# A delta-rule scan in three threads, with crosswise operands and a block-diagonal intermediate

## The chip, the cores and the metric

One core of one Trainium2 chip runs the whole program. The metric is the device time of one execution in microseconds (us). Times of single instructions are in nanoseconds (ns) or us, as the rows give them.

## The reference, cut to what matters

The reference is a network of several layers. The change lies in one part of its first block, a recurrence ("delta rule") over 256 context tokens and then 2048 tokens, for 6 heads of 64 and in two directions:

```python
def step(S, inp):
    w_t, k_t, v_t, kk_t, a_t = inp[:5]
    sa = jnp.einsum('bhvk,bhk->bhv', S, kk_t)
    S = (S * w_t[:, :, None, :] - sa[..., None] * (kk_t * a_t)[:, :, None, :]
         + v_t[..., None] * k_t[:, :, None, :])
    y = jnp.einsum('bhvk,bhk->bhv', S, inp[5]) if emit else None
    return S, y
state, ys = lax.scan(step, state, xs)
```

The state S is a 64 by 64 matrix for each head and direction. The second direction reads the tokens from the end. All numbers are fp32.

## The kernel before

`rwkv_scan` does the recurrence in 18 steps (2 of context, without output, then 16 with output). A step handles 128 tokens as two chunks of 64, for six units `u`: three groups `g` of two heads, each in two directions. Six inputs of a unit (scaled identity, alpha, rho, beta, kappa, v) lie in a tile `X`. The stages of a step, and the names used below:

- **turned** and **grams** (the fronts), once for each unit of the next step: four transposes of full 128 by 128 tiles into `gram`, a copy out by ScalarE (L1728), then 12 or 16 products of 64-row operands into `gram`, and one masked copy out by VectorE (L1759). GpSimd prepares `XE` (L1571) and the start `W` of the inverse (L1583).
- **z** and **n**, five rounds for each group: the inverse of a triangular 64 by 64 matrix for each chunk, head and direction grows by doubling. z multiplies the Gram matrix by the transposed inverse (8 matmuls of 64 by 64, 16 in the first round), ScalarE copies the result out (L1735), n multiplies that by the inverse (8 matmuls of 64 by 64, and in rounds 1 to 4 four more that make the transposed result of direction 1). VectorE writes the new entries into `W` through a mask (L1771, L1772) and transposes the other direction with one instruction (L1774).
- **x**, **p**, **f**, **s**, for each group: the solved vectors (8 matmuls with 128 moving columns), the transition matrices and gains (8 with 128 columns and 32 of 64 by 64), then the state and output of the first and of the second chunk (8 each).

`walk` sets one order for all engines: `PHASES` is the list z1 n1 z2 n2 ... z5 n5 x p f s; in each phase the three groups follow one another, and the fronts of the next step are put in at phases 0, 2, 4, 6, 8 and 9 (`AHEAD`). So a step's x, p, f and s run with nothing of the next step's rounds beside them. Each group has a PSUM pair `db[g]` of its own, and `gram` is a fourth pair shared by the fronts and the gains. The tensor engine's program is unrolled: a step is some 588 matmuls and 24 transposes. The trace shows each fp32 matmul as two pairs of LDWEIGHTS and MATMUL and each transpose as one pair. In the trace every matmul of the scan has line L1608 (the helper `mm`) and every transpose L1618.

In the rows, PE is the tensor engine's matmul, PEld its weight load; "64*64" is the part of the array that the stationary operand takes (rows*columns), and "64x128" after it is the moving operand.

Of the kernel before, what the change touches and what calls it, by code (L numbers as in the profile page):

```python
# [14 lines left out]
P = 128  # L15
# [1421 lines left out]
def rwkv_scan(nc, R, E, masks, levels, eye, ident, YR):  # L1437
# [7 lines left out]
    X_I, X_AL, X_RH, X_BE, X_KA, X_V = range(6)  # L1445
    K_AL, K_BE, K_KA, K_V, K_A, K_AR, K_KL, K_KR, K_AT, K_S0, K_Z, K_W0 = 0, 1, 2, 3, 4, 5, 6, 7, 8, 9, 10, 11
# [3 lines left out]
    PHASES = [(w, b) for b in range(1, LV) for w in "zn"] + [("x", 0), ("p", 0), ("f", 0), ("s", 0)]  # L1450
    AHEAD = {0: 0, 2: 1, 4: 2, 6: 3, 8: 4, 9: 5}

    PRODS, EVACS = 15, 18

    with ExitStack() as ctx:
        s = Scope(nc, ctx, "rsc")
        X = [[s.sb(f"X{b}{u}", [P, 6, P]) for u in range(NU)] for b in range(2)]
        XE = [s.sb(f"XE{b}", [P, 2, P]) for b in range(2)]
        TK = [[s.sb(f"TK{b}{g}", [P, 12, 2, P]) for g in range(NG)] for b in range(2)]
        W = [[s.sb(f"W{b}{g}", [P, 2, 2, P]) for g in range(NG)] for b in range(2)]  # L1460
        X12 = [s.sb(f"X12{g}", [P, 2, 2, 2, HD]) for g in range(NG)]
        PQ = [s.sb(f"PQ{g}", [P, 2, 2, 2, HD]) for g in range(NG)]
        GY = [s.sb(f"GY{g}", [P, 2, 2, 2, HD]) for g in range(NG)]
        Y = [s.sb(f"Y{g}", [P, 2, 2, HD]) for g in range(NG)]
        S = [[s.sb(f"S{a}{g}", [P, 2, HD]) for g in range(NG)] for a in range(2)]
# [4 lines left out]
        e = s.sb("e", [P, NU, 2 * CH])  # L1470
        gram = ctx.enter_context(nc.psum_tensor("rsc_gram", [P, 2, NT], F32))
        db = [ctx.enter_context(nc.psum_tensor(f"rsc_db{g}", [P, 2, NT], F32)) for g in range(NG)]
        const_in, zeroed = s.sem("const_in"), s.sem("zeroed")
        x_in = [s.sems(f"x_in{b}", NU) for b in range(2)]
        xe_ready, tl_full, tl_done, gram_full, m4_done, s0_ready, start_ready = (
            s.sem(n) for n in ("xe_ready", "tl_full", "tl_done", "gram_full", "m4_done", "s0_ready", "start_ready"))
        prod, evac, gy_done, y_out = (s.sems(n, NG) for n in ("prod", "evac", "gy_done", "y_out"))

        def scan(step):

            for n in range(NS):
                step(n // 2, n % 2, n >= NCX)

        def after(k, b):

            return None if k == NLT // 2 and b == 1 else ((k, 1) if b == 0 else (k + 1, 0))

        def walk(k, b, emit, phase, turned, grams):

            nxt = after(k, b)  # L1490
            for i, (w, lev) in enumerate(PHASES):
                for g in range(NG):
                    phase(k, b, emit, w, lev, g)
                    if nxt and i in AHEAD and g == 0:
                        turned(*nxt, AHEAD[i])
                if nxt and i in AHEAD:
                    grams(*nxt, AHEAD[i])

# [4 lines left out]
        def rows_of(u, t):  # L1503

            return t if u == 0 else other(t)

        def alpha_rho(x, h, u, cp):

            flat = x[HEADS[h], :, :].rearrange("p a t -> p (a t)")
            if u % 2 == 0:  # L1510
                return x[HEADS[h], X_AL:X_RH + 1, CHUNKS[cp]]
            if cp == 0:
                return flat[:, X_AL * P + C:X_AL * P + 3 * C].rearrange("p (a t) -> p a t", a=2)
            return flat[:, X_AL * P:X_AL * P + 6 * C].rearrange("p (a t) -> p a t", a=2)[:, :, 0:C]

        with nc.Block() as block:
            @block.sync
            def _(sp):
                def load(b, u, src):
                    x = X[b][u]  # L1520
                    if u % 2 == 0:
                        sp.dma_start(x[:, X_AL:, :], src).then_inc(x_in[b][u], 16)
                        return
                    sp.dma_start(x[:, X_RH:, :], src[:, 1:, :]).then_inc(x_in[b][u], 16)
                    for t in CHUNKS:
                        sp.dma_start(x[:, X_AL, other(t)], src[:, 0, t]).then_inc(x_in[b][u], 16)

                for dst, src in ((mk, masks), (lv, levels), (ey, eye), (idn, ident), (e, E)):
                    sp.dma_start(dst[:], src).then_inc(const_in, 16)
                for b in range(2):  # L1530
                    for u in range(NU):
                        m, d = divmod(u, 2)
                        c = NLT + b if d == 0 else NS - 1 - b
                        load(b, u, R[c, m, d])

                def step(k, b, emit):
                    if k < NLT // 2:
                        for u in range(NU):
                            m, d = divmod(u, 2)
                            c = k * 2 + b if d == 0 else k * -2 + (NLT - 1 - b)  # L1540
                            if d == 0:
                                sp.wait_ge(evac[m], k * (2 * EVACS) + (b * EVACS + 16))
                            load(b, u, R[c, m, d])
                    if emit:
                        for g in range(NG):
                            sp.wait_ge(evac[g], k * (2 * EVACS) + (b + 1) * EVACS)
                            for d in range(2):
                                tok = k * (2 * P) + (b - 2) * P if d == 0 else k * (-2 * P) + (NS - 1 - b) * P
                                sp.dma_start(YR[d, g * P:(g + 1) * P, tok:tok + P], Y[g][:, d, :, :].rearrange("p c t -> p (c t)")).then_inc(y_out[g], 16)

                scan(step)
                for g in range(NG):
                    sp.wait_ge(y_out[g], 32 * (NLT + 1))

            @block.gpsimd
            def _(pool):
                for g in range(NG):
                    nc.gpsimd.memset(S[0][g][:], 0.0).then_inc(zeroed, 1)
                pool.wait_ge(const_in, 16 * 5)

                def scaled(k, b, u):

                    f = k * (2 * NU) + (b * NU + u)
                    x = X[b][u]
                    pool.wait_ge(x_in[b][u], (k + 1) * (16 if u % 2 == 0 else 48))
                    if f >= 2:
                        pool.wait_ge(tl_full, f - 1)
                    ends = e[:, u, k * 4 + 2 * b:k * 4 + 2 * b + 2]
                    nc.gpsimd.tensor_tensor(x[:, X_I, :].rearrange("p (c t) -> p c t", c=2), ey[:].rearrange("p (c t) -> p c t", c=2),
                                            ends.unsqueeze(2).broadcast_to([P, 2, C]), ALU.mult)  # L1570
                    nc.gpsimd.tensor_tensor(XE[u % 2][:].rearrange("p a (c t) -> p a c t", c=2),  # L1571
                                            x[:, X_BE:X_KA + 1, :].rearrange("p a (c t) -> p a c t", c=2),
                                            ends.unsqueeze(1).unsqueeze(3).broadcast_to([P, 2, 2, C]), ALU.mult).then_inc(xe_ready, 1)

                def start_of(k, b, u):

                    g, d, f = u // 2, u % 2, k * (2 * NU) + (b * NU + u)
                    pool.wait_ge(m4_done, f + 1)
                    tk = TK[b][g]
                    if d == 0:  # L1580
                        nc.gpsimd.tensor_tensor(tk[:, K_S0, d, :], tk[:, K_A, d, :], lv[:, 0, d, 0, :], ALU.mult).then_inc(s0_ready, 1)
                        pool.wait_ge(s0_ready, k * NU + b * NG + g + 1)
                    nc.gpsimd.tensor_tensor(W[b][g][:, d, :, :], tk[:, K_S0:K_AT - 1:-1, d, :], ey[:].unsqueeze(1).broadcast_to([P, 2, P]),  # L1583
                                            ALU.add).then_inc(start_ready, 1)

                def fronts(k, b):
                    scaled(k, b, 0)
                    scaled(k, b, 1)
                    for u in range(NU):
                        start_of(k, b, u)  # L1590
                        if u + 2 < NU:
                            scaled(k, b, u + 2)

                def step(k, b, emit):
                    nxt = after(k, b)
                    if nxt:
                        fronts(*nxt)

                fronts(0, 0)
                scan(step)  # L1600

            @block.tensor
            def _(pe):
                pe.wait_ge(const_in, 16 * 5)
                pe.wait_ge(zeroed, NG)

# [3 lines left out]
                def turned(k, b, u):  # L1610

                    f = k * (2 * NU) + (b * NU + u)
                    x = X[b][u]
                    pe.wait_ge(xe_ready, f + 1)
                    if f:
                        pe.wait_ge(m4_done, f)
                    for j, src in enumerate((x[:, X_AL, :], XE[u % 2][:, 0, :], XE[u % 2][:, 1, :], x[:, X_V, :])):
                        t = nc.tensor.transpose(gram[:, 0, j * P:(j + 1) * P], src, idn[:])  # L1618
                    t.then_inc(tl_full, 1)

                def grams(k, b, u):

                    f = k * (2 * NU) + (b * NU + u)
# [2143 lines left out]
```

## Time and profile before

| | |
|---|---|
| median of 3 runs | 5550.07 us (5545.63 to 5558.74) |
| profiled execution | 5547.89 us, its span 5546.1 us |
| the scan in the span | its transfers are issued from 982.3, first z at 1016.8, last output at about 1681.0 |
| one step in the steady part (1166.2 to 1650.5, 13 steps) | 37.25 us |

The profiled execution's own time is 1.8 us more than its span. It lies 2.2 us under the median. The scan is an eighth of the span, and nothing else of the program runs beside it: a barrier closes each stage.

### The profile page before, as it was taken

Reading aid. Unit: us, or ns where it says so; the run is one execution under the profiler, and the core shown is the slowest. Engines: PE = TensorE matmul, PEld = TensorE weight load, DVE = VectorE, ACT = ScalarE, POOL = GpSimd, SP = SyncE. Lnnn points to the kernel's source line nnn. Section 1 sums busy time; section 2 is a strip of 40 time slices with the busy share of each in tenths; the row PEclk is TensorE's granted clock in tenths of the full one; section 3 lists DMA queues with packets and bytes.
Section 4 is the critical chain, followed back from the end, with each engine's and each line's share of the span. In section 5 each row is a group of like instructions: output and inputs, shape, how many; then the busy total and the mean of one; then the engine's idle time right before and its main releaser. Section 6 shows DMA issues by size and latency. Waiting matters only on the chain. (4 is left out here: it accounts for less than half of the span.)

```text
span 5546.1 us, 120203 instructions
## 1 busy us (share of the span) xinstructions
PE 4903.5 (88%) x51393; PEld 3755.2 (68%) x51393; DVE 3398.0 (61%) x5671; ACT 1866.0 (34%) x3105; POOL 1317.3 (24%) x1186
## 2 busy tenths in 40 slices
PE   5999999788887975979998679999897999979989
PEld 2788888677776863858886434444486888766767
DVE  5166566455557875867981678888654000258877
ACT  3244444233335432341111334444404000136642
POOL 4111111322320000350000047767535111000012
PEclk7999999899999987989999779999998999979999
DMA  8244344221211124643324310000364112220145
GB/s 291 84 140 165 140 144 144 93 72 59 69 58 67 51 71 170 209 127 97 113 94 158 114 46 18 24 18 14 108 194 128 70 67 75 98 96 34 41 130 159
DMA packets 446893, 561.50 MB, mean 101 GB/s; under 512 B 83022, under 2 KB 338010, under 8 KB 434346
## 3 DMA queue, kind: packets, MB, share of 16 engines
q1 hardware_dynamic: 376444, 366.28, 21.3%
q10 hardware_dynamic: 54622, 130.36, 6.1%
q0 software_dynamic: 15312, 57.45, 2.6%
q8 instruction: 391, 6.41, 0.5%
q14 instruction: 124, 1.02, 0.1%
HBM read 350.86 MB, written 203.12 MB: 100 GB/s over the span
## 5 line engine op out<-in xcount | busy, mean ns | idle before, releaser
L164 PE MATMUL p_bank<-p_hT_high,p_w_high 128*128 128x512 f32 (+1 forms) x2744 | 1037.7, 378 | 8.7 <-PEq L37 7.8
L166 PE MATMUL p_bank<-p_hT_high,p_w_low 128*128 128x512 f32 (+1 forms) x2744 | 1029.5, 375 | 0.0
L165 PE MATMUL p_bank<-p_hT_low,p_w_high 128*128 128x512 f32 (+1 forms) x2744 | 1029.4, 375 | 0.0
L164 PEld LDWEIGHTS p_bank<-p_hT_high,p_w_high 128*128 128x128 f32 x2744 | 517.4, 189 | 110.4 <-issue 17.5
L166 PEld LDWEIGHTS p_bank<-p_hT_high,p_w_low 128*128 128x128 f32 x2744 | 517.3, 189 | 93.9
L165 PEld LDWEIGHTS p_bank<-p_hT_low,p_w_high 128*128 128x128 f32 x2744 | 517.5, 189 | 91.6
L3011 POOL TENSOR_TENSOR at_acc<-at_acc,at_p 128x512 f32<-128x512 f32 x256 | 414.6, 1619 | 124.8 <-ACT at_p L2947 102.0
L2947 ACT ACTIVATE at_p<-at_sc 128x1024 f32<-128x1024 f32 (+1 forms) x296 | 284.7, 1013 | 378.9 <-PE at_sc L2838 373.0
L3053 DVE TENSOR_REDUCE at_mx<-at_mb 128x2 f32<-128x1024 f32 (+1 forms) x280 | 342.1, 1222 | 51.0 <-PE at_mb L2849 50.8
L164 PE MATMUL o_bank<-o_w_high,o_m_high 128*128 128x512 f32 x800 | 314.4, 393 | 64.6 <-POOL o_m_low L158 64.6
L1050 DVE COPY p_o<-p_bank 128x512 f32<-128x512 f32 (+1 forms) x52 | 33.8, 651 | 466.7 <-PE p_bank L166 466.7
L165 PE MATMUL o_bank<-o_w_low,o_m_high 128*128 128x512 f32 x800 | 313.4, 392 | 0.0
L166 PE MATMUL o_bank<-o_w_high,o_m_low 128*128 128x512 f32 x800 | 313.3, 392 | 0.0
L1608 PE MATMUL rsc_db<-rsc_W,rsc_TK 64*64 64x64 f32 x8640 | 277.0, 226 | 36.1 <-issue 18.1
L2870 PE MATMUL at_ob<-at_p,at_V 128*64 128x512 f32 (+1 forms) x1184 | 283.4, 599 | 0.7 <-ACT at_osb L2954 0.7
L1608 PEld LDWEIGHTS rsc_db<-rsc_W,rsc_TK 64*64 64x64 f32 x8640 | 230.7, 136 | 76.8 <-issue 43.9
L2837 PE MATMUL at_sc<-at_Q,at_K 128*128 128x512 f32 (+1 forms) x592 | 247.3, 419 | 1.5 <-DMA at_Q<-attention_tops 1.5
L413 ACT COPY p_o<-p_bank 128x512 f32<-128x512 f32 (+1 forms) x147 | 82.2, 560 | 476.6 <-PE p_bank L166 467.2
L3085 DVE TENSOR_TENSOR at_acc<-at_acc,at_p 128x512 f32<-128x512 f32 x256 | 205.2, 802 | 55.5 <-ACT at_p L2947 49.1
L2838 PE MATMUL at_sc<-at_Q,at_K 128*128 128x512 f32 (+1 forms) x592 | 232.1, 393 | 0.0
L164 PEld LDWEIGHTS o_bank<-o_w_high,o_m_high 128*128 128x128 f32 x800 | 151.8, 190 | 98.5 <-POOL o_m_low L158 66.9
L1759 DVE TENSOR_TENSOR rsc_TK<-rsc_gram,rsc_mk 128x640 f32<-128x640 f32 x108 | 96.3, 891 | 193.6 <-PE rsc_gram L1608 193.6
(434 smaller groups left out, 9986.0 us busy)
## 6 DMA issues: line engine op xcount, KB each, us to landing
pT<-p_o ACTq DMA_DIRECT2D x128, 256.0 KB, 2.1
rwkv_chunks<-p_arr POOLq DMA_DIRECT2D x54, 512.0 KB, 5.3
o_z<-pT SPq DMA_DIRECT2D x50, 512.0 KB, 5.3
o_y<-y SPq DMA_DIRECT2D x50, 512.0 KB, 6.6
pT<-p_eo ACTq DMA_DIRECT2D x96, 256.0 KB, 2.0
rsc_X<-rwkv_chunks SPq DMA_DIRECT2D x54, 320.0 KB, 3.4
x<-o_o ACTq DMA_DIRECT2D x32, 512.0 KB, 2.7
o_x<-x SPq DMA_DIRECT2D x32, 512.0 KB, 4.6
```

The costliest lines, as they stand in the source:

```text
L164: nc.tensor.matmul(out, lhs[0], rhs[0], start=start, stop=False)
L165: nc.tensor.matmul(out, lhs[0], rhs[1], start=False, stop=False)
L166: return nc.tensor.matmul(out, lhs[1], rhs[0], start=False, stop=stop)
L1608: return nc.tensor.matmul(out, l, r, start=start, stop=stop)
L1759: nc.vector.tensor_tensor(dst, src, mk[:, u % 2, 0:items, :].unsqueeze(1).broadcast_to([P, 2, items, C]), ALU.mult).then_inc(m4_done, 1)
L2837: nc.tensor.matmul(sc[t % 2][:, h, 0:n], K1[kv][:, keys], Q1[b % NBUF][:, h, 0:n], start=True, stop=False)
L2838: m = nc.tensor.matmul(sc[t % 2][:, h, 0:n], K2[kv][:, keys], Q2[b % NBUF][:, h, 0:n], start=False, stop=True)
L2870: m = nc.tensor.matmul(ob[h * HD:(h + 1) * HD, 0:n], V[:, tiles[j], kv * HD:(kv + 1) * HD], pr[t % 4][:, h, 0:n], start=(j == 0), stop=(t ...
L2947: nc.scalar.activation(pr[t % 4][:, :, 0:n], sc[t % 2][:, :, 0:n], ACT.Exp, scale=SC).then_inc(exp_done, 1)
L3011: nc.gpsimd.tensor_tensor(acc[b % 2][:, 1, 0:n], acc[b % 2][:, 1, 0:n], pr[t % 4][:, 1, 0:n], ALU.add).then_inc(sum_b, 1)
L3053: r = nc.vector.reduce_max(mx[b % 2][:, :, t:t + nt, c], top_bank(m)[:, :, 0:nt * n].rearrange("p h (j k) -> p h j k", j=nt), AX)
L3085: nc.vector.tensor_tensor(acc[b % 2][:, 0, 0:n], acc[b % 2][:, 0, 0:n], pr[t % 4][:, 0, 0:n], ALU.add).then_inc(sum_a, 1)
```

## The change

The scan is rewritten; the rest of the program and the other constants stay.

- **Three threads.** The order is now by slots, 15 a step. Slot j asks for item i (`asked`, the old z), finishes item i-1 (`grown`, the old n), does one ninth of the previous step's `solved`, `moves`, `gains` (slots 0 to 8) or its `state` for one chunk and all groups (slots 9 and 10), and from slot 3 on one transposition or one `grams` of the next step.
- **Block diagonal.** The intermediate goes to `ZB`, 128 by 128 for each direction and head, with the two chunks on the diagonal and zeros elsewhere. `grown` is 4 matmuls with this full 128 by 128 stationary and 64 moving columns, in place of 12 (8 in the last round) of 64 by 64. The four extra products are gone: VectorE transposes direction 1 with two more instructions of 64 rows.
- **Crosswise operands.** The keys are loaded into zero-padded places so that `grams` uses 64 by 128 stationaries (4 with 128 columns, 8 of 64 by 64) and `gains` 16 matmuls with 128 rows, in place of 32.
- PSUM: two pairs `inv[i % 2]` for the rounds, `db` for the rest, `gram` for the fronts. `X` has three buffers, filled by 30 transfers a step in place of 12. `state` and the outputs are done for all groups at once, `GY`, `Y` and `S` are one tile each.

```diff
+                def asked(i):
+                    n, lev, g = item(i)
+                    tk, wt, d = TK[n % 2][g], W[n % 2][g], inv[i % 2]
...
+                        pe.wait_ge(w_ready, i - NG + 1)
+                    if i >= 2:
+                        if item(i - 2)[1] == LV - 1:
+                            pe.wait_ge(w_ready, i - 1)
+                        else:
+                            pe.wait_ge(n_taken, taken(i - 1))
+                    for h in range(2):
+                        for u in range(2):
+                            for cp, t in enumerate(CHUNKS):
+                                z = other(t)
+                                to = rows_of(u, t)
+                                last = mm(d[to, u, h * P + to.start:h * P + to.stop], tk[z, K_M + 2 * cp, u, HEADS[h]], wt[z, u, 1, HEADS[h]])
...
-                    elif w == "n":
-                        pe.wait_ge(evac[g], done + 3 * lev - 2)
-                        for h in range(2):
-                            if lev < LV - 1:
-                                for t in CHUNKS:
-                                    at = 5 * P + h * HD
-                                    mm(flat[t, at:at + HD], wt[other(t), 1, 0, HEADS[h]], tk[other(t), K_Z, 1, HEADS[h]])
-                            for u in range(2):
-                                for z in CHUNKS:
-                                    at = 3 * P * u + h * HD
-                                    last = mm(flat[z, at:at + HD], tk[z, K_Z, u, HEADS[h]], wt[z, u, 0, HEADS[h]])
+                def grown(i):
+                    n, lev, g = item(i)
+                    wt, d = W[n % 2][g], inv[i % 2]
+                    pe.wait_ge(z_taken, i + 1)
+                    for h in range(2):
+                        for u in range(2):
+                            at = (2 + u) * P + h * HD
+                            last = mm(d[:, 0, at:at + HD], ZB[g][:, u, h, :], wt[:, u, 0, HEADS[h]])
+                    last.then_inc(n_full, 1)
...
+                        for cp, h in LANES:
+                            mm(db[HEADS[h], cp, u * P:u * P + HD], tk[:, K_E + cp, u, HEADS[h]], tk[:, K_V + cp, u, HEADS[h]])
+                        for cp, h in LANES:
+                            last = mm(db[HEADS[h], cp, u * P + HD:(u + 1) * P], tk[:, K_V + cp, u, HEADS[h]], tk[:, K_M + 1 + 2 * cp, u, HEADS[h]])
...
+                for n in range(NS + 1):
+                    for j in range(NI):
+                        i = n * NI + j
+                        if n < NS:
+                            asked(i)
+                        if 1 <= i <= NS * NI:
+                            grown(i - 1)
+                        if n:
+                            g, part = divmod(j, 3)
+                            if j < FIRST_HALF:
+                                (solved, moves, gains)[part](n - 1, g)
+                            elif j <= SECOND_HALF:
+                                state(n - 1, j - FIRST_HALF)
+                        if j >= FRONTS_AT and n + 1 < NS:
+                            u, part = divmod(j - FRONTS_AT, 2)
+                            (turned, grams)[part](n + 1, u)
...
+                def asked(i):
+                    n, lev, g = item(i)
+                    act.wait_ge(z_full, i + 1)
+                    last = nc.scalar.copy(ZB[g][:].rearrange("p u h t -> p u (h t)"), inv[i % 2][:, :, 0:2 * P])
...
+                def grown(i):
+                    n, lev, g = item(i)
+                    dve.wait_ge(n_full, i + 1)
+                    wt = W[n % 2][g]
+                    new = inv[i % 2][:, 0, 2 * P:4 * P].rearrange("p (u t) -> p u t", u=2)
+                    made = nc.vector.copy_predicated(wt[:, :, 0, :], lv[:, lev, :, 0, :].bitcast(mybir.dt.uint32), new)
...
+                    made.then_inc(n_taken, 1)
+                    dve.wait_ge(n_taken, taken(i + 1))
+                    nc.vector.transpose(wt[:, 0, 1, :], wt[:, 0, 0, :])
+                    for t in CHUNKS:
+                        last = nc.vector.transpose(wt[other(t), 1, 1, :], wt[t, 1, 0, :])
+                    last.then_inc(w_ready, 1)
```

The transfers of the first two units are now issued ahead of the constants, those of the other four after them. All engines still wait for all five constants before they begin. In the first step the fronts run two units at a time on the two pairs `db` and `gram`.

## Rows read from the trace of the kernel before

**Rows 1.** Busy time by stretch: first step, 13 steady steps, last step, next stage.

```profile
core 0: us, PE busy (x) PEld busy (x) DVE busy (x) ACT busy (x) POOL busy (x), PEclk, DMA share, GB/s
1016.80:1053.10 36.30, 31.32 (x1164) 27.59 (x1156) 19.75 (x57) 12.69 (x27) 13.86 (x26) 0.91 0.12 34
...
1166.20:1650.50 484.30, 411.12 (x15603) 363.74 (x15601) 263.95 (x782) 163.03 (x351) 146.37 (x269) 0.99 0.22 64
1650.50:1681.30 30.80, 23.56 (x1012) 21.42 (x1008) 16.48 (x58) 9.18 (x21) 0.00 (x0) 1.00 0.07 20
1700.00:2050.00 350.00, 305.51 (x9888) 274.72 (x9888) 296.96 (x626) 169.08 (x313) 0.00 (x0) 0.96 0.10 37
```

**Rows 2.** Waits of PE, steady stretch, then next stage: us, times, longest.

```profile
PE rsc_db L1608 <- issue: 35.9, 37, 2.5
PE rsc_db L1608 <- DVE rsc_W L1774: 11.7, 33, 0.5
...
PE hg_sc L2192 <- issue: 4.9, 4, 2.3
```

**Rows 3.** DMA queues, steady stretch, then next stage: packets, MB, share.

```profile
q8 instruction: 122, 2.00, 1.7%
...
q8 instruction: 78, 1.28, 1.5%
```

**Rows 4.** Timeline of PE, start and duration: a z, four transposes, two z.

```profile
1323.28 0.46 PE L1608 MATMUL rsc_db<-rsc_W,rsc_TK 64*64 64x64 f32 x16 [0.26 <-DVE rsc_W L1774]
1323.67 0.33 PE L1618 MATMUL rsc_gram<-rsc_idn,rsc_X 128*128 128x128 f32 x1
...
1324.26 0.93 PE L1608 MATMUL rsc_db<-rsc_W,rsc_TK 64*64 64x64 f32 x32
```

**Rows 5.** Timeline of PE: gains of one group, then states of the step's end.

```profile
1344.28 0.29 PE L1608 MATMUL rsc_gram<-rsc_TK 64*64 64x64 f32 x8
...
1345.21 0.62 PE L1608 MATMUL rsc_db<-rsc_TK,rsc_X 64*64 64x128 f32 x16
...
1352.29 0.27 PE L1608 MATMUL rsc_db<-rsc_S,rsc_PQ 64*64 64x64 f32 x1 [1.72 <-issue]
...
1353.04 0.45 PE L1608 MATMUL rsc_db<-rsc_S,rsc_PQ 64*64 64x64 f32 x8
...
1353.51 0.45 PE L1608 MATMUL rsc_db<-rsc_S,rsc_PQ 64*64 64x64 f32 x8
```

**Rows 6.** Weight loads by form: 128 columns, 64 columns.

```profile
L3402 PEld LDWEIGHTS na_tb<-na_idn,na_rep 128*128 128x128 f32 x128 | 19.3, 191 | 0.0
...
L1608 PEld LDWEIGHTS rsc_db<-rsc_W,rsc_TK 64*64 64x64 f32 x8640 | 230.7, 136 | 76.8 <-issue 43.9 <-DVE rsc_W L1774 24.5
```

**Rows 7.** A later stage, 5067.38 to 5067.56: matmuls by form, weight loads by time.

```profile
L3386 PE MATMUL na_win<-na_k,na_q 64*128 64x64 f32 x4 | 0.3, 244 | 0.0
...
5067.39 0.42 PEld L3386 LDWEIGHTS na_win<-na_k,na_q 64*128 64x128 f32 x6 [0.24 <-issue]
```

**Rows 8.** Timeline of PE in the next stage: 128 rows, then 64 rows.

```profile
1745.81 0.46 PE L2219 MATMUL hg_yb<-hg_P,hg_KI 128*64 128x64 f32 x10
...
1746.20 0.34 PE L2180 MATMUL hg_sc<-hg_KI 64*64 64x64 f32 x8
```

**Rows 9.** Groups of VectorE and ScalarE by form, 1120 to 1650: busy us, mean ns.

```profile
L1772 DVE COPY_PREDICATED rsc_W<-rsc_lv,rsc_db 128x256 f32<-128x256 uint32 x176 | 76.4, 434 | 0.0
...
L1774 DVE STREAM_TRANSPOSE rsc_W<-rsc_W 128x128 f32<-128x128 f32 x177 | 52.4, 296 | 0.0
L1728 ACT COPY rsc_TK<-rsc_gram 128x512 f32<-128x512 f32 x88 | 51.6, 586 | 40.7 <-PE rsc_gram L1618 40.7
...
L1759 DVE TENSOR_TENSOR rsc_TK<-rsc_gram,rsc_mk 128x768 f32<-128x768 f32 x44 | 42.1, 958 | 50.2 <-PE rsc_gram L1608 50.2
```

**Rows 10.** Timeline of the scan's start: a transfer's issue, GpSimd's first work, first z.

```profile
989.19 0.43 SPq L1524 DMA_DIRECT2D rsc_X<-rwkv_chunks  x1
...
991.12 0.40 POOL L1569 TENSOR_TENSOR rsc_X<-rsc_ey,rsc_e 128x128 f32<-128x128 f32 x1 [8.32 <-DMA rsc_X<-rwkv_chunks]
...
1016.82 0.65 PE L1608 MATMUL rsc_db<-rsc_W,rsc_TK 64*64 64x64 f32 x16
```

More of the change, by code:

```diff
@@ L1475, in rwkv_scan @@
[L1475 to L1497, printed above, removed]
+        const_in, zeroed, cleared = s.sem("const_in"), s.sem("zeroed"), s.sem("cleared")
+        x_in = [s.sems(f"x_in{b}", NU) for b in range(3)]
@@ L1589, in fronts @@
+                nc.gpsimd.memset(S[0][:], 0.0).then_inc(zeroed, 1)
+                pool.wait_ge(const_in, 16 * 5)
+                for n in range(NS):
+                    scaled(n, 0)
+                    scaled(n, 1)
                     for u in range(NU):
-                        start_of(k, b, u)
+                        start_of(n, u)
                         if u + 2 < NU:
[L1592 to L1597, printed above, removed]
@@ new lines, in solved @@
+                def solved(n, g):
+                    tk, wt = TK[n % 2][g], W[n % 2][g]
+                    pe.wait_ge(w_ready, n * NI + NI - NG + g + 1)
+                    if g:
+                        pe.wait_ge(gy_ready, n * NG + g)
+                    elif n:
+                        pe.wait_ge(st_ready, 2 * n)
+                        if emitted(n):
+                            pe.wait_ge(y_ready, 2 * emitted(n))
+                    for h in range(2):
+                        for u in range(2):
+                            for t in CHUNKS:
+                                z = rows_of(u, t)
+                                last = mm(db[other(t), u, h * P:(h + 1) * P], wt[z, u, 0, HEADS[h]], pair(tk, z, h, u, K_AL, K_W0, 1))
+                    last.then_inc(x12_full, 1)
@@ L1720, in _ @@
-                scan(lambda k, b, emit: walk(k, b, emit, phase, turned, grams))
+                                at = g * P + u * HD
+                                last = mm(db[q, 0, at:at + HD], PQ[g][q, u, cp, 0, :], S[x][q, g, u, :])
+                    last.then_inc(st_full, 1)
+                    if n < NCX:
+                        return
+                    if x:
+                        pe.wait_ge(y_ready, 2 * emitted(n) + 1)
+                    for g in range(NG):
+                        for u in range(2):
+                            cp = x if u == 0 else 1 - x
+                            for q in HEADS:
+                                at = g * P + u * HD
+                                last = mm(db[q, 1, at:at + HD], S[x][q, g, u, :], PQ[g][q, u, cp, 1, :])
@@ new lines, in gains @@
+                def gains(n, g):
+                    act.wait_ge(gy_full, n * NG + g + 1)
+                    nc.scalar.copy(GY[:, g, :, :].rearrange("p (c x) k -> p c (x k)", c=2), db[:, :, 0:2 * P]).then_inc(gy_ready, 1)
+                act.wait_ge(const_in, 16 * 5)
+                for u in range(NU):
+                    turned(0, u)
+                for n in range(NS + 1):
+                    for j in range(NI):
+                        if n < NS:
+                            asked(n * NI + j)
+                        if n and j < FIRST_HALF and j % 3 != 1:
+                            (solved, None, gains)[j % 3](n - 1, j // 3)
+                        if j >= FRONTS_AT and n + 1 < NS and (j - FRONTS_AT) % 2 == 0:
+                            turned(n + 1, (j - FRONTS_AT) // 2)
@@ new lines, in _ @@
+                for x in range(2):
+                    nc.vector.memset(inv[x][:], 0.0).then_inc(cleared, 1)
+                dve.wait_ge(const_in, 16 * 5)
+                for u in range(NU):
+                    grams(0, u)
+                for n in range(NS + 1):
+                    for j in range(NI):
+                        i = n * NI + j
+                        if 1 <= i <= NS * NI:
+                            grown(i - 1)
+                        if n and j < FIRST_HALF and j % 3 == 1:
+                            moves(n - 1, j // 3)
+                        elif n and FIRST_HALF <= j <= SECOND_HALF:
+                            state(n - 1, j - FIRST_HALF)
+                        if j >= FRONTS_AT and n + 1 < NS and (j - FRONTS_AT) % 2:
+                            grams(n + 1, (j - FRONTS_AT) // 2)
```

407 lines of the change are left out of this document (192 added, 215 removed).

## The prediction

> **What bounds the kernel now.** I read the busy times by stretch first, then PE's waits, then the timeline record by record. In the steady part a step takes 484.3 / 13 = 37.25 us, with PE busy 85%, its loads 75%, VectorE 55%, ScalarE 34% and the DMA engines 22% [rows 1]. The scan hangs on PE. The waits say what PE lacks: of what is listed most is "issue", time in which it waited for no engine (35.9 us in 37 waits), and only 11.7 us is for the transposed inverse from VectorE [rows 2].
>
> What "issue" is, the DMA queues show. In that stretch PE issued 31,204 records (matmuls and loads) and the instruction queue moved 122 packets in 2.00 MB [rows 1, 3]: one block of 16 KB for each 256 records, every 3.97 us. The next stage takes 78 blocks for 19,776 records, one every 4.49 us [rows 1, 3], and there PE's largest issue wait is 4.9 us in 350 [rows 2]. In the scan a phase of dense small matmuls ends in a stop within a group, as before 1352.29 [rows 5]. I take these stops for PE running ahead of its instruction blocks: at 3.97 us a block it starves, at 4.49 hardly.
>
> So a step is PE's own work plus stops. **Prices of a group**, from its start to the next one's start, without stops:
> - z: its 16 records begin within 0.46 - 0.22 = 0.24 us (0.22 is the length of one record), and four transposes follow 0.39 after its start [rows 4]. Two z groups take no more than 0.28 each. The first-round z (twice the matmuls) is then 0.51.
> - Four transposes: 1323.67 to 1324.26, 0.59 [rows 4].
> - Eight matmuls on only two of the array's four squares (f, s, and also n, which has four on each diagonal square): 1353.04 to 1353.51, 0.47 [rows 5]. That is 8 records a square, 0.058 each.
> - The 32 small ones of the gains: 1344.28 to 1345.21, 0.93 [rows 5]; eight with 128 columns, over four squares, twice a z's streaming: 0.43.
> - grams: 12 or 16 matmuls, eight of them with 128 columns: 0.60 or 0.71 by the same prices.
>
> A step of before: 12 z 3.4, 3 first z 1.5, 15 n 7.0, transposes 6 x 0.7 = 4.2 (with the 0.11 more ahead of them), grams 3.9, x 1.3, p 3 x 1.40 = 4.2, f and s 2.8. Sum 28.3. The other 9.0 us are stops: some 6 for instructions and 3 for data. Both are what the change can win.
>
> **What it adds: the full stationary.** `grown` has 4 matmuls of 2 records instead of 12, but each loads 128 columns. A load of 128 columns takes 191 ns, one of 64 takes 136 [rows 6]: 55 ns for 64 columns, so 0.11 us for 128. Streaming 64 columns takes 0.058. The one place of the trace with 64 moving columns behind 128-column loads shows which counts: around 5067.4 six loads of two row halves, three in each, take 0.42 us, so begin (0.42 - 0.19) / 2 = 0.115 apart, while the matmuls between them stream only 64 columns [rows 7]. Hence 8 x 0.11 = 0.88 for `grown`, against 0.47. Bounds: 0.47, if the loads were hidden, and 8 x (0.11 + 0.058) = 1.34, if load and stream followed one another; rows 7 are the nearest, I take 0.88. Over 15 items this adds 6.2 us to a step.
>
> The Trainium skill (TensorE: Matmul & The Clock Gate, What overlaps and what doesn't) says that a weight load overlaps a running matmul only if their row groups differ; by it the 1.34 would hold, and the step would be 7 us longer again. Rows 7 speak against it: loads of the same 64 rows are 0.115 apart with a stream between.
>
> **What it adds: changes of shape.** From 64-row matmuls to the full array the next group begins 0.39 - 0.24 = 0.15 after the last record's start, against some 0.04 between like groups [rows 4]. The way back costs the same: in the next stage 128-row records end at 1746.27, so the last began at 1746.05, and 64-row ones begin at 1746.20, 0.15 later [rows 8]. Each such change is 0.1 over the stream. Every item now has one ahead of `grown`, and most slots one behind it. gains become 128-row, so that in slots 2, 5, 8, 11 and 13 the second change falls away or comes later. I count 15 more ahead of `grown` and 12 behind: about 2.7 us. Four more 64 by 64 matmuls in three of six grams: 0.3.
>
> **The slots**, in us. asked 0.39 (first round 0.62); grown 1.02 with a change of shape behind it, 0.88 without; solved or moves 0.43; gains 0.98; state with outputs 1.42 (24 matmuls on two squares, 0.058 x 24); transposes 0.59, or 0.73 behind 64-row work; grams 0.71. Slots 0 and 1: 2.07 each; 2: 2.57; 3: 2.54; 4: 2.56; 5: 2.84; 6: 2.56; 7: 2.54; 8: 3.08; 9: 3.57; 10: 3.56; 11 and 13: 1.86; 12 and 14: 2.13. Sum 37.9.
>
> **Waits that replace the old ones.** `asked` of slot j+1 needs the pair `inv` that `grown` of slot j read out: its last matmul, 0.06 of semaphore, 0.434 for the masked copy [rows 9], 0.06. In slots 0, 1, 11 and 13 too little lies behind `grown`: 0.1 each, 0.45 in all. VectorE per item: 0.434 and three transposes of at most 0.296 [rows 9], 1.32; twelve of these, 3 x 0.43, and 16 other copies of at most 0.96 make 32.5, under 37.9, and `w_ready` is asked for two slots later. Without that cover each 0.1 late would cost 0.1 a slot. ScalarE: 15 copies of 0.59, 6 x (0.59 + 0.3), 9 more of 0.4 and 6 of 0.59 or less: some 22, hidden; `moves` asks for its result a slot later. GpSimd drops one instruction a group, hidden before and after. SP issues 32 transfers a step instead of 18, each at some 0.45 [rows 10]: 14.4 us of 38, and they run up to three steps ahead; the same bytes in smaller pieces, at 22% of the DMA engines [rows 1], stay hidden.
>
> **Instructions.** A step has 420 matmuls and 24 transposes, 1728 records instead of 2400: 6.75 blocks. At 38 us that is one every 5.6 us, well above the 4.49 that hardly stops [rows 3]; the densest slots (0 to 2: 368 records in 6.7 us) stay at 4.7. I leave 0.3 of the 6. Step: 37.9 + 0.45 + 0.3 = 38.6, against 37.25. The 16 middle steps, of which the first two make no outputs (half of each `state` slot, 1.4 a step): 16 x 38.6 - 2.9 = 614.7, against 1650.5 - 1053.1 = 597.4 [rows 1]: +17.
>
> **The ends.** Start: GpSimd begins at 991.1, the first z comes at 1016.8 [rows 10], 25.7 later. Now the largest constant is issued behind ten transfers (10 x 0.45), so work begins some 4.5 later, and the six fronts go in three pairs of 4.8 (two chains side by side at the low clock): first z at about 1011, 6 less. First step, nothing of a previous one beside it: 15 x 2.05 = 31 instead of 36.3 [rows 1], 5 less. Last step, 30.8 before [rows 1]: now 33 without fronts, then solved, moves, gains three times one after another with no cover (5.3 each) and the state (4.5 with the last grown), 20: 53, so 22 more. Together +11. **Sum**: 17 + 11 = +28 on the profiled execution's 5547.9 is 5576. The median of the three runs lies 2.2 above that execution, so the prediction, which is for such a median, is 5578.
>
> **Rivals.**
> - *Loads hidden* (0.12). `grown` streams at 0.058 a record: 0.47, -6.2 a step. 17 steps give -105: 5473, faster. For it: loads are prefetched elsewhere. Against: rows 7. It decides as soon as a record costs less than 0.095, where the step falls under 37.
> - *Changes of shape are free* (0.14), because they fall together with stops: -2.4 x 17 = -41, 5537, faster by a hair.
> - *The pair `inv` is late everywhere* (0.10), by 0.25 a slot, since VectorE does fronts, moves and rounds in one queue: +3.75 x 17, 5642.
> - *Instruction stops stay* (0.09) at some 0.65 a block: 6.75 x 0.65 - 0.3 = +4.1 a step, 5648. For it: I inferred their cause. The Trainium skill (Runtime: NRT & Kernel Launch, Instruction fetch mechanics) has the fetch of a block mostly hidden; by that the 6 us would be another cost, which fewer records need not remove. The rhythm in rows 3 speaks against that.
> - *Load and stream in a row* (0.05): +0.46 x 15 x 17, 5695.
> - The forecast (0.50): 5578, its own range 5558 to 5602, from 1 us a step either way less some of the ends.
>
> **How the numbers follow.** Within 0.2% (5539 to 5561, about what a measurement tells from no change) lie the low edge of the forecast and half of the free-shape case: 0.14. Faster: the hidden loads, the other half, and a little of the edge: 0.25. Slower: the rest, 0.61. The range leaves out the two outer cases (0.12 and 0.05): 5525 to 5655.
>
> **What would show it.** Records of L1608's successor with 128*128 and 64 columns begin 0.11 apart and a `grown` takes 0.88; PE's issue waits nearly vanish; the instruction queue moves some 120 blocks over the whole scan; slots of 1.9 to 3.6 us; a step of 38.6; a tail of 20 us with PE mostly idle. Wrong if the loads are 0.06 apart, or if PE waits on VectorE in every slot.

## The result and the profile after

The changed kernel takes 5653.66 us (median of 4 runs, 5644.85 to 5680.3), the kernel before in the same job 5551.77 (4 runs): ratio 1.0202, 95% interval 1.0185 to 1.0218, 102 us more. The profiled execution has a span of 5655.9 against 5546.1. Busy time by stretch, first step, 13 steady steps, last step with rounds, and the tail (the last solved to state with nothing beside them), to be held against [rows 1]:

```profile
core 0: us, PE busy (x) PEld busy (x) DVE busy (x) ACT busy (x) POOL busy (x), PEclk, DMA share, GB/s
1020.29:1053.91 33.62, 30.18 (x578) 26.23 (x576) 22.59 (x56) 14.60 (x30) 10.21 (x19) 1.00 0.22 57
1134.39:1675.63 541.24, 535.25 (x11246) 466.86 (x11240) 358.66 (x871) 254.02 (x546) 129.14 (x234) 1.00 0.23 60
1717.27:1753.10 35.83, 33.41 (x709) 29.63 (x701) 22.38 (x61) 14.14 (x30) 0.73 (x1) 0.97 0.05 14
1753.10:1782.50 29.40, 20.11 (x297) 16.89 (x297) 5.39 (x12) 5.18 (x12) 0.00 (x0) 0.51 0.00 1
```

A steady step takes 541.24 / 13 = 41.63 us instead of 37.25, with 28% fewer records, and PE is busy 99% instead of 85%. The tail runs at a granted clock of 0.51, the 1.2 GHz level. The instruction queue and PE's waits of the 13 steps:

```profile
q8 instruction: 89, 1.46, 1.1%
...
PE rsc_gram L1617 <- DVE rsc_TK L1813: 4.0, 13, 0.3
```

89 blocks are one every 6.08 us, and no wait for "issue" is left (35.9 us in the largest row of [rows 2]). So the step is longer though the stops are gone: PE's own groups cost more. Three slots of PE's timeline (L1605 is the helper `mm`, L1617 a transpose):

```profile
1307.28 1.20 PE L1605 MATMUL rsc_db<-rsc_TK 128*64 128x64 f32 x32
1308.41 0.46 PE L1605 MATMUL rsc_inv<-rsc_W,rsc_TK 64*64 64x64 f32 x16
1308.80 1.10 PE L1605 MATMUL rsc_inv<-rsc_W,rsc_ZB 128*128 128x64 f32 x8
1309.84 0.67 PE L1605 MATMUL rsc_db<-rsc_TK,rsc_W 64*64 64x128 f32 x16
1310.44 0.33 PE L1617 MATMUL rsc_gram<-rsc_idn,rsc_X 128*128 128x128 f32 x1
...
1311.02 0.46 PE L1605 MATMUL rsc_inv<-rsc_W,rsc_TK 64*64 64x64 f32 x16
1311.41 1.10 PE L1605 MATMUL rsc_inv<-rsc_W,rsc_ZB 128*128 128x64 f32 x8
1312.45 0.67 PE L1605 MATMUL rsc_db<-rsc_TK,rsc_XA 64*64 64x128 f32 x16
1313.05 1.11 PE L1605 MATMUL rsc_gram<-rsc_X 64*128 64x128 f32 x24
1313.97 0.41 PE L1605 MATMUL rsc_inv<-rsc_W,rsc_TK 64*64 64x64 f32 x16
```

From start to start: gains 1308.41 - 1307.28 = 1.13, `asked` 0.39, `grown` 1.04, solved or moves 0.60, transposes 0.58, `grams` 0.92. The rows follow each other without a gap; the step is the sum of such groups.

**Where the time went**, from the scan's first GpSimd instruction (982.31, now 985.07) to its last output:

| part | before | after | difference | forecast |
|---|---|---|---|---|
| start, to the first z | 34.5 | 35.2 | +0.7 | -6 |
| first step | 36.3 | 33.6 | -2.7 | -5 |
| 16 middle steps | 597.4 | 663.4 | +66 | +17 |
| last step and tail | 30.8 | 65.2 | +34.4 | +22 |

That is +98 of the spans' 110. The other 12 lie where the programs are the same: 3 ahead of the scan, 9 behind it.

### The profile page after: what moved, and what is told of

It is laid out like the page before. It is cut to its first block and busy times, and to the rows that moved or that the text cites. A ratio compares the mean times of both kernels' runs of the same rounds, so it can differ in the third digit from the quotient of the medians.

```text
span 5655.9 us, 108993 instructions
## 1 busy us (share of the span) xinstructions
PE 5092.2 (90%) x45345; PEld 3914.9 (69%) x45345; DVE 3531.4 (62%) x5801; ACT 1991.7 (35%) x3375; POOL 1292.7 (23%) x1130
## 5 line engine op out<-in xcount | busy, mean ns | idle before, releaser
L1050 DVE COPY p_o<-p_bank 128x512 f32<-128x512 f32 (+1 forms) x52 | 33.8, 651 | 466.8 <-PE p_bank L166 466.8
L1605 PE MATMUL rsc_inv<-rsc_W,rsc_ZB 128*128 128x64 f32 x2160 | 299.8, 282 | 0.5 <-ACT rsc_TK L1778 0.5
L1605 PEld LDWEIGHTS rsc_inv<-rsc_W,rsc_ZB 128*128 128x128 f32 x2160 | 262.9, 192 | 18.8 <-ACT rsc_TK L1778 0.7
L1820 DVE COPY_PREDICATED rsc_W<-rsc_lv,rsc_inv 128x256 f32<-128x256 uint32 x270 | 120.5, 446 | 204.5 <-PE rsc_inv L1605 202.2
```

Source lines behind the costliest of these rows:

```text
L1605: return nc.tensor.matmul(out, l, r, start=start, stop=stop)
L1820: made = nc.vector.copy_predicated(wt[:, :, 0, :], lv[:, lev, :, 0, :].bitcast(mybir.dt.uint32), new)
```

## The experiments

Each edit is shown against the changed kernel, cut. The theory P to be tested: a record with 128 stationary columns costs PE 0.11 us, whatever it streams, and a change between a 64 and a 128 column stationary costs some 0.1 to 0.15 us wherever it stands. The rivals stand in the expectations.

**1. `grown` in squares (e1_squares).** The zeros of the block diagonal are skipped: 8 matmuls of 64 by 64.

```diff
-    last = mm(d[:, 0, at:at + HD], ZB[g][:, u, h, :], wt[:, u, 0, HEADS[h]])
+    for z in CHUNKS:
+        last = mm(d[z, 0, at:at + HD], ZB[g][z, u, h, z], wt[z, u, 0, HEADS[h]])
```

> The changed kernel with one part undone: grown again works in 64 by 64 squares, 8 matmuls on the two diagonal blocks in place of 4 with the full 128 by 128 stationary. Theory P (the tensor engine is the bound, and the full stationary costs it 0.11 us a record in loads plus a change of array shape on either side): in the trace of the changed kernel an item takes 0.83 us inside grown, 0.148 ahead of it and 0.205 behind; in squares it should be some 0.41, 0.04 and 0.04 (0.15 before transposes and gains). That is about 10 us less a step of 41.63, less 0.6 for waits on the pair inv that come out in slots with little cover: a step of about 32.2, and 5654 - 17 x 9.4 = 5494 us. Theory V (the rounds are held by VectorE's and ScalarE's turn in the loop, the tensor engine only looks busy): the step stays above 38 us, the time above 5590. Theory F (instruction blocks): 1968 records a step are 7.7 blocks; at the 3.97 us a block of the kernel before that is a floor of 30.5 us, so stops inside groups come back in dense places and cost 0 to 2 us a step.

5538.54 us, ratio 0.9962 (0.9946 to 0.9978). Thirteen steps, and the group with its neighbours:

```profile
1119.33:1574.36 455.03, 417.59 (x12805) 362.08 (x12800) 351.40 (x871) 252.95 (x546) 129.42 (x234) 1.00 0.27 71
...
1302.84 0.63 PE L1605 MATMUL rsc_inv<-rsc_W,rsc_ZB 64*64 64x64 f32 x16
1303.31 0.67 PE L1605 MATMUL rsc_db<-rsc_TK,rsc_XA 64*64 64x128 f32 x16
```

`grown` falls from 1.04 to 0.47, a step to 35.0. This one edit turns the change from 2.0% slower into 0.4% faster: undoing the full stationary, with the changes of shape around it, wins 6.6 us a step, and what is left of the change 2.3 against the kernel before. Theory P had expected more, a step of 32.2. PE's busy time did fall by 9.1 us a step ((535.25 - 417.59) / 13), but PE now waits for VectorE's copies, 2.5 us a step:

```profile
PE rsc_gram L1617 <- DVE rsc_TK L1814: 15.7, 26, 0.7
PE rsc_db L1605 <- DVE rsc_PQ L1837: 13.9, 26, 0.6
PE rsc_inv L1605 <- DVE rsc_W L1821: 2.8, 14, 0.2
```

**2. `grown` twice (e2_twice).** Each of its four matmuls is issued two times.

```diff
+    for _again in range(2):
         last = mm(d[:, 0, at:at + HD], ZB[g][:, u, h, :], wt[:, u, 0, HEADS[h]])
```

> The changed kernel with the suspected cost doubled: the four matmuls of every grown are issued twice (the second time they write the same values). Theory P: eight more records at 0.1115 us each, 0.89 us an item, all on the path: 15 x 0.89 = 13.4 us a step, 55.0 us in place of 41.63, and about 5654 + 18 x 13.4 = 5895 us. If loads could hide under streams it would be 0.058 a record, 7 us a step and about 5779 us. Theory V: much of it is hidden, a step under 48 us.

5886.43 us (one run), a step of 54.78. The price by itself:

```profile
1398.68 2.00 PE L1605 MATMUL rsc_inv<-rsc_W,rsc_ZB 128*128 128x64 f32 x16
1400.61 0.67 PE L1605 MATMUL rsc_db<-rsc_TK,rsc_W 64*64 64x128 f32 x16
```

Eight more records take 2.00 - 1.10 = 0.90 more: 0.112 each, on the very rows that the record ahead streams through. So the sentence of the Trainium skill (TensorE: Matmul & The Clock Gate, What overlaps and what doesn't) that a load overlaps a running matmul only if the row groups differ doesn't hold here; by it, and the prediction's prices of load and stream, 0.17 a record was to be seen.

**3. `grams` in squares (e3_grams64).** Its four 64 by 128 stationaries become eight of 64 by 64, so the stationary's columns stay 64. More records, no other change.

```diff
-    mm(to[:, h, cp * P:(cp + 1) * P], x[HEADS[h], X_KB + cp, :], alpha_rho(x, h, u, cp))
+    for r in CHUNKS:
+        mm(to[r, h, cp * P:(cp + 1) * P], x[HEADS[h], X_KB + cp, r], alpha_rho(x, h, u, cp))
```

> The changed kernel with the crosswise stationary of grams split: eight matmuls of 64 by 64 with 128 moving columns in place of four of 64 by 128, into the same places. Theory P with changes of shape in columns too (64 by 128 to 64 by 64 costs a drain, which I had priced at nothing): grams fall from 0.89 us inside to about 0.68, 6 x 0.21 = 1.3 us a step, and the time to about 5632 us. If only a change of rows costs a drain, and the 0.89 comes from the streaming itself, nothing changes: 5654 us.

5654.99 us, ratio 1.0172 (1.0152 to 1.0193), which alone looks like no change (the intervals overlap). The trace says otherwise:

```profile
1022.25:1072.32 50.07, 48.44 (x627) 43.87 (x624) 23.06 (x56) 14.58 (x30) 10.65 (x19) 0.53 0.17 43
1151.30:1673.58 522.28, 514.57 (x11869) 460.31 (x11863) 357.30 (x871) 252.19 (x546) 129.12 (x234) 1.00 0.24 62
...
1323.49 0.67 PE L1605 MATMUL rsc_db<-rsc_TK,rsc_XA 64*64 64x128 f32 x16
1323.97 0.85 PE L1605 MATMUL rsc_gram<-rsc_X 64*64 64x128 f32 x32
1324.64 0.41 PE L1605 MATMUL rsc_inv<-rsc_W,rsc_TK 64*64 64x64 f32 x16
```

With 8 more records `grams` takes 0.67 instead of 0.92, and the moves ahead of it 0.48 instead of 0.60: a step of 40.18, 1.46 less, as P had it. But in the profiled execution the first step took 50.1 us instead of 33.6, at a granted clock of 0.53 instead of 1.00, which gives back 16 of the 23 us that 16 steps win.

**4. Both in squares (e4_sq_grams).**

> Both edits together: grown in squares and grams in squares; only transposes and gains still change the array's shape. Theory P: the gains add up, a step of about 31 us and some 5472 us, less what VectorE gives back: its own work is some 27 us a step with three dependent transposes an item, so slots with a short piece of the tensor engine's work begin to wait for the masked copy. Theory F: 2064 records, 8.1 blocks a step, floor 32 us at 3.97 a block: then this kernel is no faster than the one with grown in squares alone.

5526.31 us, ratio 0.9945 (0.9929 to 0.9962), faster than both kernels, where theory P had expected 5472. A step is 450.78 / 13 = 34.68; of the 1.46 of experiment 3 only 0.3 is left. Most of the rest went into waits: for VectorE 40.0 us in 13 steps against 32.4 in e1_squares, for "issue" 3.0 against 0.4.

**5. Transposes behind the copies (e6_late_turns, e7_sq_late).** VectorE's three transposes of an item move behind the moves or grams of its slot, in e4_sq_grams and in e1_squares.

```diff
     made.then_inc(n_taken, 1)
+def turned(i): ...  # the three transposes and w_ready
...
         grams(n + 1, (j - FRONTS_AT) // 2)
+    if 1 <= i <= NS * NI:
+        turned(i - 1)
```

> Squares for grown and grams as in the run e4_sq_grams (34.6 us a step, 5526), and VectorE does the three transposes of an item behind the moves or grams of its slot instead of ahead of them. Theory Q (order of VectorE's queue): of the 34.6 us of a step PE waits 37.3 / 13 = 2.9 for VectorE, for the copies behind the transposes (24.3 us for TK, 13.0 for PQ in 13 steps). With these copies first, most of it goes: a step of 32.2, 17 x 2.4 = 41 less, 5485. Theory F (instruction blocks): a step has 2064 records, 8.06 blocks; at the 3.97 us a block of the kernel before the step can't fall under 32.0, and stops come back: issue waits of over 1 us a step, a step of about 33, 5498. Rival A (VectorE's amount, not its order): the waits stay, 5526.

> Only grown in squares, as in e1_squares (34.9 us a step, 5538.5), with the transposes moved behind. Q: of 29.6 / 13 = 2.3 us a step of waits for VectorE's TK and PQ some 2 go: 32.8, 5503; 7.69 blocks at 4.27 us each, so by F too there is no stop. Rival A: 5538.

5542.98 us, ratio 0.9977 (0.9967 to 0.9986), and 5552.34 us, ratio 0.9997 (0.9988 to 1.0006): both worse than without the edit. Theory Q falls. PE's waits in 13 steps of e6_late_turns (two smaller rows of "issue", 1.1 and 0.6, and one of 0.4 for ScalarE are left out):

```profile
PE rsc_inv L1605 <- DVE rsc_W L1822: 25.1, 48, 0.7
PE rsc_inv L1605 <- issue: 12.7, 14, 1.3
PE rsc_gram L1617 <- DVE rsc_TK L1815: 8.8, 23, 0.5
PE rsc_db L1605 <- issue: 2.6, 5, 0.9
```

The waits for TK and PQ went (24.3 to 8.8, 13.0 to none), but the next item's masked copy now stands behind the transposes, and `asked` waits 25.1 us for it instead of 2.7. So VectorE's in-order queue handed most of the wait on, not all: in sum PE waits 33.9 us for VectorE instead of 40.0. What makes the step longer (35.46 us instead of 34.68) is the "issue", 17.0 us instead of 3.0. In e7_sq_late both grew against e1_squares: 32.4 to 40.1 for VectorE, 0.4 to 4.8 for "issue". Why "issue" grows with this order is open.

**6. Two transposes less (e9_two_turns_less).** In e4_sq_grams, VectorE leaves out the two transposes of 64 rows.

```diff
-    for t in CHUNKS:
-        last = nc.vector.transpose(wt[other(t), 1, 1, :], wt[t, 1, 0, :])
```

> e4_sq_grams without the two transposes of 64 rows of each item (the transposed inverse of direction 1 is left at its start value, so the output is not the reference's). VectorE has 12 x 0.62 = 7.4 us a step less. If PE waited for VectorE's queue, the waits go: a step of 32.2 or, with the stops of theory F, 33; 5485 to 5498. If not: 34.6, 5526.

5503.12 us (one run), a step of 33.38. PE's waits for VectorE fall from 40.0 to 14.5 us in 13 steps, but its waits for "issue" rise from 3.0 to 10.8. Less work of VectorE wins where another order did not, and the waits for "issue" come up behind it.

**7. Both ends (e8_ends, e10_sq_grams_ends, e11_changed_ends),** of e6_late_turns, of e4_sq_grams and of the changed kernel. The largest constant gets a semaphore of its own, on which VectorE waits behind the first fronts. In the last step solved, moves and gains go by stage instead of by group, in three PSUM pairs.

```diff
-    for dst, src in ((e, E), (ey, eye), (idn, ident), (mk, masks), (lv, levels)):
+    for dst, src in ((e, E), (ey, eye), (idn, ident), (mk, masks)):
         sp.dma_start(dst[:], src).then_inc(const_in, 16)
+    sp.dma_start(lv[:], levels).then_inc(lv_in, 16)
...
+    def free(n, g):
+        return db if n < NS - 1 else (db, inv[0], gram)[g]
...
-    g, part = divmod(j, 3)
+    g, part = divmod(j, 3) if n < NS else (j % 3, j // 3)
```

> e6_late_turns with two changes at the ends. Start: the largest constant (1.5 MB, used by VectorE's masked copy alone) has a semaphore of its own, so the first fronts no longer wait for it: 5 us earlier (13.8 us from the first instruction to the first work in the changed kernel, 8.8 before). Last step: solved for all three groups, then moves for all, then gains for all, each group in a PSUM pair of its own that is free by then, instead of one group after another. Theory T (the tail is a chain without cover): 24.8 us of e4_sq_grams become 1.6 + three ScalarE turns of 1.2 + 0.9 + 0.9 + 2.0 + 0.7 + 5.3 = 15, together 14 less than e6_late_turns. Rival: the tail hangs on the low clock of PE's own work, which stays: 5 less, by the start alone.

> e4_sq_grams (grown and grams in squares, transposes where the change has them) with both ends of e8_ends. The steps are e4's 34.6. If the ends add up as the two traces show them (start 5 us earlier, last step 12.8 in place of 24.8), it is 17 under e4_sq_grams: 5509, ratio 0.9914. Rival: the gain of e8_ends over e6_late_turns (23) held 6 us of something else that e4 lacks: 5503.

> The changed kernel with the two ends only; its steps keep the full stationary, 41.63 us. Start 5 us earlier; the last step of 29.4 us, which ran at a granted clock of 0.51, becomes 13 to 15: together 20 less, 5634. Rival (the low clock sets the tail and stays): 10 less, 5644.

e8_ends: 5520.1 us, ratio 0.994 (0.9927 to 0.9954), 23 under e6_late_turns, where 14 were expected; the other 9 are not explained. e10_sq_grams_ends: 5518.01 us, 0.993 (0.9917 to 0.9944). Its first step and its tail:

```profile
1012.56:1041.61 29.05, 21.94 (x740) 19.14 (x736) 22.64 (x56) 14.59 (x30) 10.66 (x19) 0.98 0.37 94
1624.91:1637.80 12.89, 10.36 (x304) 9.09 (x304) 5.20 (x12) 4.94 (x12) 0.00 (x0) 1.00 0.01 4
```

The tail takes 12.9 us at a granted clock of 1.00 instead of e4's 24.8 at 0.72, and the first z comes 29.4 us after GpSimd's first instruction instead of 33.8. In the traces the scan is 14 us shorter than e4's, near the 17 expected; the medians show 8, with intervals that overlap.

e11_changed_ends: 5664.47 us, ratio 1.0176 (1.015 to 1.0202), not the 5634 expected. The profiled execution (5667.04) has both gains, 3.8 at the start and 15.5 in the tail, and loses them in the first two steps:

```profile
1019.17:1071.39 52.22, 50.37 (x579) 44.39 (x576) 23.05 (x56) 14.60 (x30) 10.21 (x19) 0.53 0.18 46
1071.39:1116.92 45.53, 45.15 (x827) 39.92 (x825) 26.56 (x65) 19.64 (x42) 9.96 (x18) 0.85 0.18 46
...
1776.00:1789.90 13.90, 12.83 (x297) 11.68 (x297) 4.74 (x11) 4.95 (x12) 0.00 (x0) 0.82 0.01 2
```

These two steps take 52.2 + 45.5 instead of 33.6 + 40.2, 24 us more, with the clock at 0.53 and 0.85. The steps behind them are the changed kernel's 41.63. The four runs were 5667.04, 5664.2, 5664.74 and 5633.46: the last is the expected time. Its mean granted clock over the whole program was 0.948, that of the other three as 0.942, 0.942 and 0.939, so I take it for one in which the clock was up from the start; no trace shows it.

**8. An order between (e12_mixed).** As e10_sq_grams_ends, with only the two half transposes behind the copies.

> e10_sq_grams_ends with VectorE's order between the two tried: masked copy, one transpose, the moves or grams of the slot, then the two half transposes. Theory M: the copies for TK and PQ come 0.6 sooner and the next masked copy is only 0.3 later than needed, so of the 2.9 us a step of waits 1 goes: 5492. Rival R (one queue, any delay only moves the wait, as e6_late_turns showed with +17): the same as e10 or up to 17 more, 5509 to 5526.

5512.0 us, ratio 0.992 (0.9905 to 0.9935), the lowest of the kernels that compute all, but its interval overlaps that of e10_sq_grams_ends. Waits for VectorE fell from 40.0 to 27.2 us in 13 steps, those for "issue" rose from 5.0 to 16.6: a step of 34.95 against 34.82. The step came out as rival R had it, but not for R's reason: the waits for VectorE fell by 1 us a step, as theory M had it, and "issue" took it back.

**9. Half the columns a record (e13_half_stream).**

```diff
-    last = mm(d[:, 0, at:at + HD], ZB[g][:, u, h, :], wt[:, u, 0, HEADS[h]])
+    for c in (0, HD // 2):
+        last = mm(d[:, 0, at + c:at + c + HD // 2], ZB[g][:, u, h, :], wt[:, u, 0, h * HD + c:h * HD + c + HD // 2])
```

> The changed kernel with each of grown's four matmuls cut into two of 32 moving columns, each with the whole 128 by 128 stationary. Loads double, the streamed columns stay. Theory L (128 columns of load set a record's 0.111): 8 records more at 0.111, as in e2_twice, a step of 54.8, 5886. Rival S (a record is its stream plus about 0.054 beside it): 16 x (0.029 + 0.054) = 1.33 for grown, a step of 49.1, 5785.

6375.84 us (one run), which neither theory gave. Two groups and five stretches of 20 us:

```profile
1373.29 3.62 PE L1605 MATMUL rsc_inv<-rsc_W,rsc_ZB 128*128 128x32 f32 x16
...
1463.47 1.97 PE L1605 MATMUL rsc_inv<-rsc_W,rsc_ZB 128*128 128x32 f32 x16
...
1180.00:1200.00 20.00, 20.00 (x208) 18.12 (x208) 6.86 (x20) 4.49 (x10) 0.00 (x0) 0.50 0.13 34
1260.00:1280.00 20.00, 20.00 (x219) 19.16 (x220) 4.23 (x10) 3.60 (x9) 2.59 (x5) 0.50 0.04 10
1300.00:1320.00 20.00, 20.00 (x347) 17.94 (x344) 9.61 (x24) 7.79 (x16) 3.31 (x6) 0.93 0.15 37
1360.00:1380.00 20.00, 20.00 (x192) 17.79 (x188) 5.82 (x15) 4.49 (x11) 1.66 (x3) 0.50 0.16 41
1460.00:1480.00 20.00, 20.00 (x366) 18.16 (x366) 10.55 (x26) 7.24 (x16) 4.96 (x9) 1.00 0.24 64
```

At full clock 16 records of 32 columns take 1.97, as 16 of 64 columns do (2.00): the load sets the price, theory L. But much of the time PE is granted the lower level (a mean of 0.63 from 1200 to 1700), with PE busy in all of each stretch shown, and there the group takes nearly twice as long. That is where the 490 us above theory L come from.

## Why the prediction was wrong

5578 was forecast, within 5558 to 5602, and 5653.66 measured. The direction held, and most of the mechanisms: the stops for instructions went, full records cost 0.112, `grown` took 1.04 against 1.02 priced before a change of shape, changes of shape cost 0.11 ahead of it. What failed is the sum of the slots, 37.9: it came to 41.6. With the 0.75 left for waits and stops the step was to be 38.6, so it is 3 us longer, 49 in the middle. The terms that were mis-sized:

- **`grams` 0.71: measured 0.92.** Six a step, 1.3 us. I took the price of records spread over four squares; with 64 by 128 stationaries it is 0.25 dearer than in squares, by experiment 3, for all its fewer records.
- **A change from 64 to 128 columns, or back, priced at nothing.** I counted changes of shape only between 64 rows and the whole array. Ahead of gains (3), behind gains (3) and between solved or moves and `grams` (2) some 0.16 is to be added, between the state and `grams` (1) 0.12: about 1.4 us. `grown` ahead of gains takes 1.04, not 0.88; gains 1.13, not 0.98; moves ahead of grams 0.60, not 0.43; the state 1.54, not 1.42. Experiment 3 takes part of them away and wins what they cost.
- **Waits for VectorE, 0.45: some 1.2.** In slots 0, 1 and 11 `asked` begins 0.14 behind the end of the masked copy, in slots 11 and 13 the transposes 0.14 behind the end of the copy to TK. The list of waits shows 0.3 of the 1.2 (4.0 / 13), because PE counts as busy while the last records of a group still run. Against these waits stand the 0.3 that I had left for instruction stops, of which none came.
- **The tail, 20 us: 29.4.** The order without cover was forecast, its clock was not: PE was busy 20.1 of these 29.4 us, and the granted clock was 0.51. By stage and at full clock the same work takes 12.9 (experiment 7).
- **The start, -6: +0.7.** Work begins 5.0 later, as priced (13.8 us behind the first instruction instead of 8.8), but the fronts take 21.4 us, where three pairs of 4.8 were to take 14.4.

For the step these are 1.3 + 1.4 + 0.75 - 0.3 = 3.15, and `asked` behind `grams`, 0.35 instead of 0.39, gives 0.1 of it back. Slot 1 shows such a wait: the moves take 0.70 from start to start instead of 0.43, and the masked copy ends at 1305.46, 0.14 ahead of `asked`:

```profile
1304.90 0.67 PE L1605 MATMUL rsc_db<-rsc_TK,rsc_XA 64*64 64x128 f32 x16
1305.60 0.46 PE L1605 MATMUL rsc_inv<-rsc_W,rsc_TK 64*64 64x64 f32 x16
...
1305.01 0.45 DVE L1820 COPY_PREDICATED rsc_W<-rsc_lv,rsc_inv 128x256 f32<-128x256 uint32 x1 [1.91 <-PE rsc_inv L1605]
```

The same shortfall lay open in the prediction's own sum for the kernel before. That sum was 28.3 us a step, and the 9.0 left to 37.25 were called stops. But PE was busy 411.12 / 13 = 31.6, and beside the two rows of [rows 2] the list of waits has these three:

```profile
PE rsc_gram L1608 <- issue: 11.1, 15, 1.8
PE rsc_gram L1618 <- DVE rsc_TK L1759: 6.8, 12, 0.6
PE rsc_gram L1608 <- ACT rsc_GY L1741: 6.0, 23, 0.3
```

All five are 71.5 / 13 = 5.5 us a step, 3.6 of them "issue". So the prices missed 3.3 us of PE's time before, and as much after (37.9 against 535.25 / 13 = 41.2). The rise of PE's own work, 9.6 us, came out as the two sums had it. What was wrong is what stood against it: not 9.0 us of stops could be won, but 5.5.

The rival "instruction stops stay" named nearly the measured time, 5648, and is refuted by the trace: right number, wrong cause. "Loads hidden" falls with experiments 1, 2 and 9, "changes of shape are free" with experiment 3, "load and stream in a row" with 2 and 9. "The pair `inv` is late everywhere" is not what cost the changed kernel its time: it is late in three slots, and all waits for VectorE are some 1.2 us a step. With a faster PE, in experiments 1 and 4, what PE waits for is mostly VectorE's other copies, TK and PQ; the masked copy leads only with the transposes moved, in experiments 5 and 8.

Why was it wrong by 102 against 28? Each group was priced by the time inside it, from its first record to its last, and the way to the next group added only where I expected it. Start to start prices, taken from pairs of neighbours of the same two shapes, would have held these 0.15s, and the busy time of the kernel before would have shown that the sum was short.

**Left open.** That the stops of before are for instruction blocks was not tried by itself. For it: at 3.97, 4.06, 4.21, 4.51 and 6.08 us a block (before, e9, e4, e1, after) the waits for "issue" in 13 steps are 47.0, 10.8, 3.0, 0.4 and 0 us. Against it as the only cause: e6_late_turns, e12_mixed and e7_sq_late have 17.0, 16.6 and 4.8 at 4.35, 4.29 and 4.65. These are the three measured so in which VectorE's transposes stand behind the copies; the number of PE's records is that of e4 and e1. The 9 us behind the scan are not explained.

## What to carry to other kernels

Zeros that are loaded into the array are not free: with 64 or 32 moving columns a record with a full stationary cost its load, 0.112 us, so a block-diagonal operand that halves the instructions doubled the time of `grown`, while the squares run side by side. Price groups from start to start, count every change of the stationary's rows or columns between neighbours, and hold the sum against the engine's busy time before calling the rest a wait. When PE gets faster, look at the in-order queue that feeds it next: here moving its work about won nothing, and less work did, as did another order of the stages at the end.

## What the runs showed of the hardware

**A busy PE at half clock.** In e13_half_stream PE is busy for all of 20 us at a granted clock of 0.50, the 1.2 GHz level; ahead of that and in it, it mostly loads full stationaries and streams 32 columns behind each. In e2_twice, otherwise the same sequence with 64 columns, the 13 steps have a clock of 1.00. The first step shows it too: of the five profiled executions with the full stationary three had it at a low clock (e3, e11, e13), of the eight with squares none (all 26.5 to 30.5 us). In e3 and e11 the low clock takes back 16 and 24 us. Times scatter as well: the four runs of the changed kernel lie 35 us apart, those of e11_changed_ends 34, those of each kernel with squares at most 19; that the first steps' clock is behind it is not shown. The Trainium skill (TensorE: Matmul & The Clock Gate, What's actually happening) has activity release the throttle; here the lower level stayed for stretches of 20 us with PE's records back to back.

**Weight loads of the same rows overlap the stream ahead of them**, 0.112 us a record of 128 columns at full clock, with 64 or 32 columns streamed behind it, and nearly twice that at the lower level (1.97 and 3.62 for 16).

**More records can be faster.** The 8 squares of e1_squares' `grown` and the 16 matmuls of e3_grams64's `grams` beat fewer larger ones: 16 records in 0.47 instead of 8 in 1.04, 32 in 0.67 instead of 24 in 0.92.
